# Attention: the first four turned tiles copied by ScalarE in two halves, each with its own signal

## The chip, the cores and the metric

The kernel runs on one core of a Trainium2 chip. The metric is the device time of one execution in microseconds, the median over runs. Before the change three runs gave 2184.6, 2189.52 and 2190.21 us, median 2189.52.

## What is computed

One encoder layer for two sequences of 272 and 1040 rows (16 meta rows are put ahead of 256 and of 1024), all in fp32. After a norm and a joint projection, one half of the width goes through a bidirectional RWKV-7 recurrence and the other through differential attention; both are projected, added, and followed by a gated feed-forward block. The part that matters here is the attention of 4 heads:

```python
s = jnp.einsum('bqhcd,bkhcd->bhcqk', qb, k)      # c = 0, 1: two score maps a head
pr = jax.nn.softmax(s, axis=-1)
amap = pr[:, :, 0] - lam * pr[:, :, 1]
return jnp.einsum('bhqk,bkhe->bqhe', amap, v)    # 128 columns of v
```

## The kernel before, in words

The stage is the function `attention`. A unit is 128 queries of one head. Each head has ten units: two of the short sequence (272 keys, "short units") and eight of the long one (1040 keys, "long units"), so there are 40 units, 8 short and 32 long, in the order short, short, long x8, four times over. Nothing reorders them: each engine runs a list of instructions written out by hand, and semaphores tie the lists together.

For unit k TensorE makes the two score maps (`score`, L1957) in two areas of PSUM, pS0 and pS1. VectorE takes the row maximum of each (`largest`, L2047), ScalarE the exponential with its row sum (`exp`, L2003: an ACTIVATE and a read of the accumulator), and VectorE the difference of the two maps (`difference`, L2054 to L2058), which gives the 128 x keys matrix in `pr`. For the product with v the keys must lie on the partitions, so TensorE turns the matrix in tiles of 128 x 128 (`turn`, L1970) into PSUM, from where the tiles are copied to `amT` in SBUF; then TensorE multiplies tile by tile with v and adds up in pO (`times_v`, L1980). Each fp32 matmul of `times_v` is recorded as two passes, each with a weight load.

A long unit has nine tiles in three batches, `tiles_of`: 0 to 3, 4 to 6, and 7 with 8 (tile 8 has 16 keys). Batch 0 is turned into the bank pT and copied by ScalarE (`turn_copy`, L1923 for full tiles, L1926 for the 16 keys of a short unit's last tile). Batches 2 and 1 are copied by VectorE (`tail`, the same lines): batch 2 from pT, batch 1 from the free end of pS0. A short unit has one batch of three tiles, copied by ScalarE with two instructions (two tiles, then 16 keys) and one signal behind the second.

TensorE's order in one turn of its loop is: scores of k (they need both exponentials of k - 1), batch 0 of k - 1 turned (needs the difference), product of batch 0 (needs ScalarE's copy and a free half of pO), batch 2 turned, batch 1 turned (needs the first exponential of k, since it writes into pS0), product of batch 2 (needs VectorE's copies), product of batch 1. ScalarE's order is: copy of batch 0 of k - 1, two exponentials of k, copy of the finished output of k - 1 (L2014). VectorE's order is: difference of k - 1, from unit 24 on one transpose of the solved inverse (L2068, L2070), two maxima of k, then the copies of batches 2 and 1 of k - 1.

Beside this, POOL works on the solve of the recurrence (`substitute`, L1032 to L1045) for the first part of the stage. The block of the next stage starts when all engines have left this one.

Of the kernel before, what the change touches and what calls it, by code (L numbers as in the profile page):

```python
# [26 lines left out]
P = 128  # L27
D = 1024
META = 16
LEN_A, LEN_B = META + 256, META + 1024  # L30
# [102 lines left out]
PRIMED = 2  # L133
# [1731 lines left out]
def attention(nc, g):  # L1865

    units = []
# [7 lines left out]
    units = [(h,) + u for h in range(HEADS) for u in units]  # L1875
    ALL = len(units)
    with Ctx(nc, "at") as c:
        ident = c.sb("ident", (P, P))
        pr = [[c.sb(f"pr{s}{x}", (P, LEN_B)) for x in range(2)] for s in range(2)]
        amT = [c.sb(f"amT{s}", (P, 9, P)) for s in range(2)]  # L1880
# [6 lines left out]
        pT, pO = c.ps("pT"), c.ps("pO")  # L1887
# [6 lines left out]
        turned, act_copied, tail_copied = c.sem("turned"), c.sem("act_copied"), c.sem("tail_copied")  # L1894
        tiles_of = [[range(0, 4), range(4, 7), range(7, 9)] if u[3] == LEN_B else [range(0, 3)] for u in units]
        batches = [len(x) for x in tiles_of]
        by_act = [min(n, 1) for n in batches]
        by_dve = [n - a for n, a in zip(batches, by_act)]
        bat0, act0, dve0 = ([sum(x[:k]) for k in range(ALL)] for x in (batches, by_act, by_dve))
        row_sum = lambda k, x: st[k % 2][:, 1, 1:2] if x else g.z0[:, units[k][0], k % NU:k % NU + 1]  # L1900
        out_cols = lambda k: slice(k % 2 * P, (k % 2 + 1) * P)

        AFTER = (0, 2, 1)

        def copied(eng, k, b):

            if b == 0:
                eng.wait_ge(act_copied, PRIMED + act0[k] + 1)
            else:
                eng.wait_ge(tail_copied, PRIMED + dve0[k] + AFTER[b])  # L1910

        def turned_tile(b, w):

            return pS[0][:, 2 * 512 + (w - 3) * P:2 * 512 + (w - 2) * P] if b == 1 else pT[:, w % 7 * P:(w % 7 + 1) * P]

        def copy_batch(copy, k, b):

            ln = units[k][3]
            tiles = tiles_of[k][b]
            full = min(tiles.stop, ln // P)  # L1920
            src = pS[0][:, 2 * 512 + P:3 * 512] if b == 1 else pT[:, :]
            n = full - tiles.start
            last = copy(amT[k % 2][:, tiles.start:full, :], src[:, 0:n * P].rearrange("p (w t) -> p w t", w=n))  # L1923
            if full < tiles.stop:
                kn = ln - full * P
                last = copy(amT[k % 2][0:kn, full, :], turned_tile(b, full)[0:kn, :])  # L1926
            return last

        with nc.Block() as block:
            @block.sync  # L1930
            def _(sp):
                c.prime(sp)
                sp.dma_start(ident[:, :], g.small_of("ident")).then_inc(ident_in, 16)
                sp.dma_start(lam[:, :], g.lambdas.partition_broadcast(P)).then_inc(lam_in, 16)
                for sem, n in g.solve_stored:
                    sp.wait_ge(sem, n)
                for q in (1, 3):
                    sp.dma_start(g.below_first[QUADS[q], :, :].rearrange("p u c -> p (u c)"), g.below[q // 2, :, 0]).then_inc(first_in, 16)
                sp.wait_ge(first_in, PRIMED + 32)
# [6 lines left out]
            @block.tensor  # L1946
            def _(pe):
                mm = nc.tensor.matmul

                def score(k):  # L1950
                    h, q0, a, ln, v0 = units[k]
                    for x in range(2):
                        pe.wait_ge(exped[x], PRIMED + k)
                    for lo in range(0, ln, 512):
                        hi = min(lo + 512, ln)
                        for x, rows in enumerate(HALVES):
                            last = mm(pS[x][:, lo:hi], g.qr[rows, h, q0:q0 + P], g.kr[rows, h, a + lo:a + hi],  # L1957
                                      start=True, stop=True)
                            if hi == ln:
                                last.then_inc(scores[x], 1)  # L1960

                def turn(k, b):
                    ln = units[k][3]
                    if b == 0:
                        pe.wait_ge(diffed, PRIMED + k + 1)
                    if b == 1 and k + 1 < ALL:
                        pe.wait_ge(exped[0], PRIMED + k + 2)
                    for w in tiles_of[k][b]:
                        kn = min(P, ln - w * P)
                        last = nc.tensor.transpose(turned_tile(b, w)[0:kn, :], pr[k % 2][0][:, w * P:w * P + kn], ident[:, :])  # L1970
                    last.then_inc(turned, 1)

                def times_v(k, b):
                    h, q0, a, ln, v0 = units[k]
                    if b == 0:
                        pe.wait_ge(ocopied, PRIMED + k - 1)
                    copied(pe, k, b)
                    for w in tiles_of[k][b]:
                        kn = min(P, ln - w * P)
                        last = mm(pO[:, out_cols(k)], amT[k % 2][0:kn, w, :], g.vt[0:kn, h, v0 + w, :],  # L1980
                                  start=(w == 0), stop=(w == tiles_of[k][min(1, batches[k] - 1)][-1]))
                    if b == min(1, batches[k] - 1):
                        last.then_inc(outs, 1)
                score(0)
                pe.wait_ge(ident_in, PRIMED + 16)
                for k in range(1, ALL + 1):
                    if k < ALL:
                        score(k)
                    if k:
                        turn(k - 1, 0)  # L1990
                        times_v(k - 1, 0)
                        if batches[k - 1] > 1:
                            turn(k - 1, 2)
                            turn(k - 1, 1)
                            times_v(k - 1, 2)
                            times_v(k - 1, 1)

            @block.scalar
            def _(act):
                def exp(k, x):  # L2000
                    ln = units[k][3]
                    act.wait_ge(maxed[x], PRIMED + k + 1)
                    nc.scalar.activation(pr[k % 2][x][:, 0:ln], pS[x][:, 0:ln], ACT.Exp,  # L2003
                                         bias=st[k % 2][:, x, 0:1], accum_out=row_sum(k, x)).then_inc(exped[x], 1)

                def turn_copy(k, b):
                    act.wait_ge(turned, PRIMED + bat0[k] + b + 1)
                    if b == 0:
                        act.wait_ge(outs, PRIMED + k - 1)
                    copy_batch(nc.scalar.copy, k, b).then_inc(act_copied, 1)  # L2010

                def out_of(k):
                    act.wait_ge(outs, PRIMED + k + 1)
                    nc.scalar.copy(g.o_rows[:, units[k][0], k % NU, :], pO[:, out_cols(k)]).then_inc(ocopied, 1)  # L2014
                for k in range(ALL + 1):
                    if k:
                        turn_copy(k - 1, 0)
                    if k < ALL:
                        exp(k, 0)
                        exp(k, 1)  # L2020
                    if k == 0:
                        act.wait_ge(lamb, PRIMED + 1)
                        nc.scalar.activation(lams[:, 0:2], lams[:, 0:2], ACT.Exp).then_inc(lamb, 1)
                    if k:
                        out_of(k - 1)
# [1230 lines left out]
```

## Time and profile before

| | |
|---|---|
| median of three runs | 2189.52 us |
| the profiled execution | 2189.49 us, span 2187.7 us |
| TensorE's mean granted clock | 0.952 |
| attention stage | from about 649 to 927 us of the span |
| TensorE, VectorE, ScalarE busy in 649 to 927 | 231.0, 201.9, 116.8 us of 278 |
| long unit that repeats | 7.08 us |
| ScalarE's copies of batch 0 | 40, of 372 to 586 ns |

The busy time is a mean over stages with different limits. Times in a timeline are from the span's start; an entry with "x8" merges eight instructions that follow each other in the same group, and its duration is the time they took together.

### The profile page before, as it was taken

What the parts mean: (1) busy time and instruction counts of PE and PEld (TensorE: products, weight loads), DVE (VectorE), ACT (ScalarE), POOL (GpSimd) and SP (SyncE); (2) the same over time, 40 slices, a digit from 0 to 9 for tenths busy, and PEclk for the clock granted to TensorE, in tenths of its full rate; (3) what the DMA queues carried; (4) which work ended last, traced back from release to release, by engine and by line L of the source; (5) the groups of instructions that cost most, each with busy time, mean ns of one, the idle gap of its engine ahead of it and who ended that gap; (6) DMA issues with size and microseconds to landing.
All of it is one profiled execution on the core that took longest, in us unless ns stands there. A gap on an engine that the chain in (4) does not pass through costs nothing. (4 is left out here: it accounts for less than half of the span.)

```text
span 2187.7 us, 40777 instructions
## 1 busy us (share of the span) xinstructions
PE 1998.1 (91%) x16199; PEld 1666.5 (76%) x16199; DVE 1426.5 (65%) x2329; ACT 959.5 (44%) x1790; POOL 348.1 (16%) x354
## 2 busy tenths in 40 slices
PE   5999999997768888878999698899999999999999
PEld 4666777776545555677887487899999999988887
DVE  5877667674866678766777646765555555557566
ACT  7454467773744444444444322422322333333433
POOL 0000000000019994074453200000000000000000
PEclk8999999998878999958999899899999999999999
DMA  4111157777940000029983543022222222295343
GB/s 180 66 45 49 62 205 260 255 264 273 291 145 1 1 1 1 7 87 187 198 179 93 184 133 135 29 105 88 105 81 87 89 93 81 90 352 168 100 147 109
DMA packets 152296, 274.88 MB, mean 126 GB/s; under 512 B 13264, under 2 KB 85840, under 8 KB 149936
## 3 DMA queue, kind: packets, MB, share of 16 engines
q1 hardware_dynamic: 152112, 272.34, 39.1%
q8 instruction: 127, 2.08, 0.4%
q14 instruction: 57, 0.47, 0.1%
HBM read 169.39 MB, written 99.93 MB: 123 GB/s over the span
## 5 line engine op out<-in xcount | busy, mean ns | idle before, releaser
L2964 DVE TENSOR_TENSOR ff_lefts<-normed_raw,ff_lefts 128x512 fp32r<-128x512 f32 x154 | 105.5, 686 | 98.3 <-ACT ff_lefts L2848 98.3
L224 PE MATMUL ff_acc<-right_t_low,ff_lefts 128*128 128x320 f32 x528 | 163.1, 309 | 0.0
L225 PE MATMUL ff_acc<-right_t_high,ff_lefts 128*128 128x320 f32 x528 | 163.1, 309 | 0.0
L223 PE MATMUL ff_acc<-right_t_high,ff_lefts 128*128 128x320 f32 x528 | 163.1, 309 | 0.0
L223 PE MATMUL ff_acc<-normed_nl 128*128 128x512 f32 x385 | 149.8, 389 | 0.0
L225 PE MATMUL ff_acc<-normed_nl,normed_nh 128*128 128x512 f32 x385 | 149.8, 389 | 0.0
L2848 ACT CAST ff_lefts<-normed_raw 128x512 fp32r<-128x512 f32 x154 | 93.5, 621 | 116.0 <-DMA normed_raw<-in_w_up 56.1
L1980 PE MATMUL at_pO<-heads_vt,at_amT 128*128 128x128 f32 (+1 forms) x624 | 104.5, 302 | 34.8 <-ACT at_amT L1923 24.5
L2874 ACT COPY normed_n<-ff_acc 128x640 f32<-128x640 f32 x66 | 45.8, 694 | 205.5 <-PE ff_acc L225 204.4
L1980 PEld LDWEIGHTS at_pO<-heads_vt,at_amT 128*128 128x128 f32 (+1 forms) x624 | 82.8, 195 | 60.9 <-issue 39.9
L3036 DVE TENSOR_TENSOR normed_nl<-normed_raw,normed_nh 128x640 fp32r<-128x640 f32 x77 | 63.4, 823 | 91.7 <-ACT normed_nh L2897 91.7
L2897 ACT CAST normed_nh<-normed_raw 128x640 fp32r<-128x640 f32 x77 | 56.2, 730 | 143.6 <-PE ff_acc L225 123.9
L223 PE MATMUL pj_acc<-parts_nh,pj_w0rest 128*128 128x512 f32 (+1 forms) x288 | 110.2, 383 | 7.1 <-DVE parts_nl L802 7.1
L223 PE MATMUL ff_acc<-normed_nh,ff_lefts 128*128 128x320 f32 x352 | 109.8, 312 | 7.5 <-DVE ff_lefts L2964 7.5
L224 PE MATMUL ff_acc<-normed_nl,ff_lefts 128*128 128x320 f32 x352 | 109.6, 311 | 0.0
L225 PE MATMUL ff_acc<-normed_nh,ff_lefts 128*128 128x320 f32 x352 | 109.6, 311 | 0.0
L223 PE MATMUL pj_acc<-parts_nh,pj_w1rest 128*128 128x512 f32 (+1 forms) x288 | 109.5, 380 | 0.0
L2047 DVE TENSOR_REDUCE at_st<-at_pS 128x1 f32<-128x1040 f32 (+1 forms) x80 | 82.6, 1074 | 37.7 <-PE at_pS L1957 37.6
L635 ACT COPY pj_raw<-pj_acc 128x512 f32<-128x512 f32 (+1 forms) x72 | 37.4, 522 | 156.9 <-PE pj_acc L225 155.5
L224 PE MATMUL pj_acc<-parts_nl,pj_w1high 128*128 128x512 f32 (+1 forms) x288 | 105.6, 367 | 0.0
L225 PE MATMUL pj_acc<-parts_nh,pj_w1high 128*128 128x512 f32 (+1 forms) x288 | 105.4, 366 | 0.0
L224 PE MATMUL pj_acc<-parts_nl,pj_w0high 128*128 128x512 f32 (+1 forms) x288 | 105.4, 366 | 0.0
(384 smaller groups left out, 5687.9 us busy)
## 6 DMA issues: line engine op xcount, KB each, us to landing
normed_raw<-dram_h SPq DMA_DIRECT2D x77, 320.0 KB, 3.0
ch_ops<-dram_sx SPq DMA_DIRECT2D x88, 256.0 KB, 5.1
dram_sx<-pr_sx SPq DMA_DIRECT2D x16, 1024.0 KB, 4.6
dram_h<-normed_spread_h SPq DMA_DIRECT2D x44, 320.0 KB, 2.3
pj_packed<-in_w_in SPq DMA_DIRECT2D x24, 512.0 KB, 4.9
heads_vt<-dram_ab SPq DMA_DIRECT2D x44, 256.0 KB, 5.4
normed_raw<-in_w_gate SPq DMA_DIRECT2D x22, 512.0 KB, 4.4
normed_raw<-in_w_up SPq DMA_DIRECT2D x22, 512.0 KB
```

The source lines that it names most:

```text
L223: nc.tensor.matmul(out, ll, rh, start=start, stop=False, skip_group_check=onto_kept)
L224: nc.tensor.matmul(out, lh, rl, start=False, stop=False, skip_group_check=onto_kept)
L225: return nc.tensor.matmul(out, lh, rh, start=False, stop=stop, skip_group_check=onto_kept)
L635: nc.scalar.copy(raw[p % 2][:, CUTS[n]:CUTS[n + 1]], acc[bank_of(i)][:, 0:widths[n]]).then_inc(copied, 1)
L1980: last = mm(pO[:, out_cols(k)], amT[k % 2][0:kn, w, :], g.vt[0:kn, h, v0 + w, :], start=(w == 0), stop=(w == tiles_of[k][min(1, batches[k] ...
L2047: nc.vector.reduce_max(st[k % 2][:, x, 0:1], pS[x][:, 0:ln], AX_X, negate=True).then_inc(maxed[x], 1)
L2848: nc.scalar.copy(lefts[:, q % LEFTS, 0, :], raw[:, y, QUARTER[p], :]).then_inc(high, 1)
L2874: nc.scalar.copy(in_two(to), got(y, p)).then_inc(kept, 1)
L2897: nc.scalar.copy(left_high[s], left_raw[s]).then_inc(left_cut, 1)
L2964: tt(lefts[:, q % LEFTS, 1, :], raw[:, y, QUARTER[p], :], lefts[:, q % LEFTS, 0, :].bitcast(F32), ALU.subtract).then_inc(low, 1)
L3036: tt(left_low[s], left_raw[s], left_high[s].bitcast(F32), ALU.subtract).then_inc(left_rest, 1)
```

## The change

ScalarE copies batch 0 in two instructions for long units also: tiles 0 and 1, then tiles 2 and 3, and signals after each. For short units the two instructions are those of before (tiles 0 and 1, then the 16 keys of tile 2), with a signal after each. TensorE waits for the first signal before tile 0 and for the second before tile 2. The counters follow; the helper `copied` is gone, its wait for the tail stands in `times_v`.

```diff
--- before.py
+++ after.py
@@ -1894,20 +1894,12 @@
         turned, act_copied, tail_copied = c.sem("turned"), c.sem("act_copied"), c.sem("tail_copied")
         tiles_of = [[range(0, 4), range(4, 7), range(7, 9)] if u[3] == LEN_B else [range(0, 3)] for u in units]
         batches = [len(x) for x in tiles_of]
-        by_act = [min(n, 1) for n in batches]
-        by_dve = [n - a for n, a in zip(batches, by_act)]
-        bat0, act0, dve0 = ([sum(x[:k]) for k in range(ALL)] for x in (batches, by_act, by_dve))
+        by_dve = [n - 1 for n in batches]
+        bat0, dve0 = ([sum(x[:k]) for k in range(ALL)] for x in (batches, by_dve))
         row_sum = lambda k, x: st[k % 2][:, 1, 1:2] if x else g.z0[:, units[k][0], k % NU:k % NU + 1]
         out_cols = lambda k: slice(k % 2 * P, (k % 2 + 1) * P)
 
         AFTER = (0, 2, 1)
-
-        def copied(eng, k, b):
-
-            if b == 0:
-                eng.wait_ge(act_copied, PRIMED + act0[k] + 1)
-            else:
-                eng.wait_ge(tail_copied, PRIMED + dve0[k] + AFTER[b])
 
         def turned_tile(b, w):
 
@@ -1974,8 +1966,11 @@
                     h, q0, a, ln, v0 = units[k]
                     if b == 0:
                         pe.wait_ge(ocopied, PRIMED + k - 1)
-                    copied(pe, k, b)
+                    if b:
+                        pe.wait_ge(tail_copied, PRIMED + dve0[k] + AFTER[b])
                     for w in tiles_of[k][b]:
+                        if w in (0, 2):
+                            pe.wait_ge(act_copied, PRIMED + 2 * k + w // 2 + 1)
                         kn = min(P, ln - w * P)
                         last = mm(pO[:, out_cols(k)], amT[k % 2][0:kn, w, :], g.vt[0:kn, h, v0 + w, :],
                                   start=(w == 0), stop=(w == tiles_of[k][min(1, batches[k] - 1)][-1]))
@@ -2007,7 +2002,14 @@
                     act.wait_ge(turned, PRIMED + bat0[k] + b + 1)
                     if b == 0:
                         act.wait_ge(outs, PRIMED + k - 1)
-                    copy_batch(nc.scalar.copy, k, b).then_inc(act_copied, 1)
+                    ln = units[k][3]
+                    nc.scalar.copy(amT[k % 2][:, 0:2, :], pT[:, 0:2 * P].rearrange("p (w t) -> p w t", w=2)).then_inc(act_copied, 1)
+                    if ln == LEN_B:
+                        last = nc.scalar.copy(amT[k % 2][:, 2:4, :], pT[:, 2 * P:4 * P].rearrange("p (w t) -> p w t", w=2))
+                    else:
+                        kn = ln - 2 * P
+                        last = nc.scalar.copy(amT[k % 2][0:kn, 2, :], pT[0:kn, 2 * P:3 * P])
+                    last.then_inc(act_copied, 1)
 
                 def out_of(k):
                     act.wait_ge(outs, PRIMED + k + 1)
```

## Rows read from the trace of the kernel before

**Rows 1.** The page: busy time by engine, and the chain that ended last, by line.
```profile
PE 1998.1 (91%) x16199; PEld 1666.5 (76%) x16199; DVE 1426.5 (65%) x2329; ACT 959.5 (44%) x1790; POOL 348.1 (16%) x354
...
PE ff_acc L223 12%; PE ff_acc L225 12%; PE ff_acc L224 12%; DVE ff_lefts L2964 0%; DVE normed_n L3062 0%; ACT ff_lefts L2848 0%
```

**Rows 2.** The waits, 649 to 927 us: engine and line, releaser, total us, times, longest.
```profile
PE at_pO L1980 <- ACT at_amT L1923: 24.5, 32, 0.8
...
PEld at_pO L1980 <- DVE at_amT L1926: 12.5, 32, 0.5
...
PE at_pO L1980 <- ACT at_amT L1926: 5.6, 8, 0.7
```

**Rows 3.** Windows of single units: us, busy by engine, PEclk, DMA share, GB/s.
```profile
708.07:715.15 7.08, 6.17 (x39) 4.22 (x39) 5.10 (x9) 3.21 (x6) 6.45 (x9) 1.00 0.00 0
...
730.87:739.27 8.40, 6.16 (x22) 3.52 (x22) 5.49 (x6) 3.03 (x7) 7.85 (x8) 0.64 0.00 0
739.27:747.65 8.38, 7.61 (x39) 5.66 (x39) 5.06 (x9) 3.08 (x7) 7.91 (x7) 0.75 0.01 2
...
866.82:874.33 7.51, 5.27 (x22) 3.06 (x22) 5.21 (x7) 3.04 (x7) 0.00 (x0) 0.77 0.00 0
```

**Rows 4.** The timeline of one long unit: start us, us, engine, line, idle before.
```profile
707.48 2.39 DVE L2047 TENSOR_REDUCE at_st<-at_pS 128x1 f32<-128x1040 f32 x2 [0.71 <-PE at_pS L1957]
...
708.07 0.58 ACT L1923 COPY at_amT<-at_pT 128x512 f32<-128x512 f32 x1 [2.37 <-PE at_pT L1970]
...
708.75 1.13 ACT L2003 ACTIVATE at_pr<-at_pS,at_st 128x1040 f32<-128x1040 f32 x1
708.77 0.97 PEld L1980 LDWEIGHTS at_pO<-heads_vt,at_amT 128*128 128x128 f32 x8 [0.98 <-issue]
708.80 1.13 PE L1980 MATMUL at_pO<-heads_vt,at_amT 128*128 128x128 f32 x8 [0.77 <-ACT at_amT L1923]
...
709.77 0.38 PE L1970 MATMUL at_pT<-at_ident,at_pr 128*128 128x128 f32 x2
709.78 0.19 ACT L2003 ACTIVATION_READ_ACCUMULATOR at_pr<-at_pS,at_st 128x1 f32 x1
...
710.02 0.55 PE L1970 MATMUL at_pS<-at_ident,at_pr 128*128 128x128 f32 x3
...
710.39 0.27 DVE L1926 COPY at_amT<-at_pT 16x128 f32<-16x128 f32 x1
...
710.61 0.56 DVE L1923 COPY at_amT<-at_pS 128x384 f32<-128x384 f32 x1
710.72 1.58 PEld L1980 LDWEIGHTS at_pO<-heads_vt,at_amT 128*128 128x128 f32 x10 [0.39 <-DVE at_amT L1926]
...
711.72 1.30 DVE L2058 SCALAR_TENSOR_TENSOR at_pr<-at_pr,at_st 128x1040 f32<-128x1040 f32 x1
```

**Rows 5.** The tile that the edit copies, whole trace: durations ns min/median/max, forms.
```profile
L1923 ACT COPY at_amT<-at_pT x40: 372/585/586, 657.9 to 922.5; 128x512 f32<-128x512 f32 x32, 128x256 f32<-128x256 f32 x8
```

**Rows 6.** The timeline of two short units after each other.
```profile
726.55 0.37 ACT L1923 COPY at_amT<-at_pT 128x256 f32<-128x256 f32 x1 [0.87 <-PE at_pT L1970]
726.82 0.25 ACT L1926 COPY at_amT<-at_pT 16x128 f32<-16x128 f32 x1
...
727.82 0.19 ACT L2003 ACTIVATION_READ_ACCUMULATOR at_pr<-at_pS,at_st 128x1 f32 x1
...
728.24 2.11 PE L1957 MATMUL at_pS<-heads_kr,heads_qr 64*128 64x512 f32 x12
...
734.17 4.02 PE L1957 MATMUL at_pS<-heads_kr,heads_qr 64*128 64x512 f32 x12 [1.54 <-ACT at_pr L2003]
```

**Rows 7.** The timeline at a transpose of the inverse, and the last work of POOL.
```profile
835.49 1.16 DVE L2070 STREAM_TRANSPOSE solved_by_row<-solved_inv 128x512 f32<-128x512 f32 x1
...
836.53 2.36 DVE L2047 TENSOR_REDUCE at_st<-at_pS 128x1 f32<-128x1040 f32 x2
...
845.16 0.31 POOL L1045 TENSOR_TENSOR solved_inv<-solved_inv,solved_solve_tmp 128x62 f32<-128x62 f32 x1
```

## Prediction

> **What bounds the kernel now.** The page first: TensorE is busy for 91% of the span and the chain that ended last runs on TensorE rows of the feed-forward stage [rows 1]. That chain says nothing of the attention stage, so I read this stage by itself: its waits, then the tile that the edit touches, then one long unit and the short units in order of time. In the stage (649 to 927 us) the waits show TensorE held before the product by ScalarE's copy, 24.5 us in 32 waits for the long units and 5.6 us in 8 for the short ones, and before the tail product by VectorE's small copy, 12.5 us in 32 [rows 2]. These are the waits of TensorE on another engine that come back in every unit with a size.
>
> The repeating long unit takes 7.08 us (708.07 to 715.15) [rows 3], and 22 or so of the 32 are like it. Let T = 708.07, the start of ScalarE's 128x512 copy. TensorE waits until T + 0.73 (matmul at 708.80), issues 8 passes, the two transposes of batch 2 at 709.77, waits for the first exponential (its accumulator read ends at 709.97) and turns batch 1 at 710.02, waits for VectorE's small copies (end 710.66), and issues the tail at 710.72 [rows 4]. The difference for the next turn is done at 711.72 + 1.30 = 713.02, more than a microsecond before the next turn [rows 4]. So one chain of TensorE's own work goes round the loop with gaps in it; a gap shortened ahead of the product counts if the two later gates let it through.
>
> **The change, part by part.**
> *The copy in halves.* A 128x512 copy takes 585 ns, a 128x256 one 372 ns, both on ScalarE from the same bank [rows 5]. The product now starts on the end of the first: 585 - 372 = 213 ns earlier in each of 32 long units, with the same two waits ahead of it. The extra instruction: a copy behind a 372 ns copy starts 0.27 us after it (726.55 to 726.82) [rows 6], so two halves end at T + 0.27 + 0.37 = T + 0.64 instead of T + 0.585.
>
> *What that does to the exponential behind it on ScalarE.* The first exponential starts at 708.75 = T + 0.68, just after VectorE's first maximum (half of the 2.39 us from 707.48, so about 708.68) [rows 4]. The second half leaves ScalarE at T + 0.64, and the next instruction may start some 0.10 before that (0.37 against a spacing of 0.27). The exponential stays where it is: 0. Bounds: -0 (no overlap at all: T + 0.27 becomes T + 0.37, exponential at about T + 0.78) to 0.10 us later.
>
> *The new wait at tile 2.* Queued behind it on TensorE is everything: the rest of the product, both turns, the tail. Loads in the product are spaced (0.97 - 0.19)/7 = 0.11 us [rows 4], so tile 2's first load, the third, would be due at T + 0.70 + 0.22 - 0.21 = T + 0.71. The signal: second half at T + 0.64, plus the 0.05 that lies between the accumulator read's end (709.97) and the transposes (710.02) [rows 4] = T + 0.69. Met, by 0.02 us. I take 0; the bound is the serial copy, end T + 0.74, release T + 0.80, a stall of 0.09, and a restart on top (below).
>
 What the rows show of a restart: eight loads span 0.97 us but eight matmuls 1.13, (1.13 - 0.28)/7 = 0.12 against 0.11, and the first matmul stands 0.03 behind its load, so about 0.1 us for a restart. If every tile 2 paid this, the sum below would be 32 x 0.1 = 3.2 us smaller; with the signal before the due load it is not.
>
> *The gates behind the product.* (1) Batch 2's transposes come 0.21 earlier, 709.56 to 709.94. (2) Batch 1's transposes wait for the first exponential, unchanged at 710.02; the gap before them grows by 0.21. (3) VectorE has finished its second maximum at 709.87 and so copies batch 2 at 709.98, not 710.19; it ends at 710.45, and the tail's first load may go at 710.51. TensorE's last of the three transposes starts at 710.02 + 0.55 - 0.27 = 710.30, its next slot is 710.41: the tail starts 0.21 earlier. (4) VectorE's 384-wide copy stays at 710.61 to 711.17, signal 711.22. The tail's loads take 1.58 us for ten [rows 4]; the seventh-last of them, six before the end, stood at 712.30 - 0.19 - 5 x 0.11 = 711.55 and is now due at 711.34. Met by 0.12. So what I feared, that turn 1 takes over, does not reach the tail: the tail was held by the small copies, and those move. Gain per long unit 0.213 us. 32 x 0.213 = 6.82.
>
> *Short units.* Their old signal came after the 16-row copy (starts 0.27, takes 0.25: T + 0.52); now after the first (T + 0.37), 0.15 less. Of eight, four are followed by another short one: there the next scores start at 728.24 and also need the second exponential, whose read ends at 728.01 [rows 6]; with the 0.14 that two waits cost (708.655 to 708.80) it is 728.15, so 0.09 each, 0.36 together. The other four are followed by a long unit; the scores after them wait 1.54 us for ScalarE [rows 6], which starts its exponentials by VectorE's maximum and not by the copy: 0.
>
> *Where cover is missing.* From unit 24 on VectorE transposes a part of the inverse between the difference and the maximum. At 835.49 it takes 1.16 and the maximum starts at 836.53 [rows 7], 0.52 before the copy at 837.05 where it is 0.60 in the plain unit; a start of TensorE 0.21 earlier finds it 0.29 late, and the batch-2 copy, behind both maxima, stays where it was. This happens when POOL's work stretches VectorE's difference, and POOL ends at 845.5 [rows 7]: about three units, -0.2 each = -0.6. In plain units the transposes have 0.3 us to spare even so. No wait of VectorE on POOL stands among the waits of the stage, and three to four microseconds at that point don't bring one: after 845.5 POOL's part is complete.
>
> Sum: 6.82 + 0.36 - 0.6 = 6.6 us off the stage. The next stages start behind it as before and move as a block. The profiled execution took 2189.49 us (span 2187.7 and 1.8 around it), the median of the three runs is 2189.52: the same. 2189.5 - 6.6 = **2182.9 us**, -0.30%.
>
> **The rivals.**
> *A. Tile 2 stalls.* The halves don't overlap, or the signal is later than 0.05: stall 0.09 and a restart of 0.1, so 0.02 left of 0.213 per long unit. 32 x 0.02 + 0.4 = 1 us: 2188.5; half of it, 2186. For: the margin is 0.02. Against: the 0.27 spacing was seen in every short unit.
> *B. The exponential takes the place.* If ScalarE's second half delays the first exponential by x, turn 1 and the tail's limit move by x; 0.10 is free. At x = 0.2 half the gain is gone: 3.3 us, 2186.2. For: turn 1 starts 0.05 after its read ends [rows 4], so it waits for it already. Against: the maximum, not the copy, starts it.
> *C. The clock gives more.* After each head's short units the granted clock falls to the lower level (1.2 of 2.4 GHz). In the second head the stretch from 730.87 (a short unit's product, a long one's scores) takes 8.40 us at 0.64, the long unit after it 8.38 at 0.75, so 6.0 + 4.2 = 10.2 us low; in the fourth head the same stretch, from 866.82, takes 7.51 at 0.77 (3.4 us low) and the next is plain [rows 3]. Two heads at the shorter spell would give 2 x (0.89 + 1.30) = 4.4 more: 2178.5. For: less idle TensorE in the unit that decides. Against: the gap of 1.54 us that precedes the fall stays. The runs before lie between 2184.6 and 2190.2. The skill's same page, "What's actually happening", says that where the transition falls depends on the phase of a count that runs by itself, so the same kernel varies.
> *D. The clock takes it, slower than before.* One mechanism: the gap before turn 1 grows by 0.21 and stands nearer to the others, and in the long units of a head the clock stays low. A long unit at the lower level costs up to 1.30 more (8.38 against 7.08, only part of it low) [rows 3]; from six such units on the gain is lost, two heads of eight make +20.8 - 6.6 = +14: 2204. Against: TensorE's busy share rises, 6.17 of 7.08 us [rows 3] to 6.17 of 6.87, and in no plain unit is the clock below 1.00.
>
> **How the numbers follow.** Forecast 0.64, A 0.11, B 0.08, C 0.12, D 0.05. A measurement of this kernel can tell about 0.3% (6.6 us) from no change, and the forecast lies on that bound: 0.37 faster, 0.27 same. With C faster, A and B same, D slower: faster 0.49, same 0.46, slower 0.05. The range from 2178.5 (C) to 2187.5 (most of A and B) leaves out D and the ends of A.
>
> **What would show it.** Right: the long unit's copy-to-copy distance is 6.87 instead of 7.08 us; 64 halves at 372 ns; the product 0.52 behind the first copy; TensorE's gap before turn 1 longer by 0.2 us; the exponential still 0.68 behind T; the stage some 6.6 us shorter, others unchanged. Wrong: a wait of TensorE on ScalarE's copy between tiles 1 and 2 (A), exponentials later than T + 0.78 (B), a unit distance still near 7.08, or a granted clock below 1.00 inside a head (D).

## The result and the profile after

In the first comparison seven runs of the changed kernel gave a median of 2173.82 us (2168.34 to 2180.26) against 2189.37 before (2184.6 to 2190.66, seven runs): 15.6 us less, ratio 0.9942, 95% interval 0.9924 to 0.996. The forecast was 2182.9 and a range down to 2178.5, so the time lies below the range. Four later sets of runs on other occasions gave 0.9965, 0.9951, 0.9957 and 0.9948. Over all runs the kernel before took 2185.5 us in the mean (141 executions) and the changed one 2176.0 (47): 9.5 us less, with a 95% interval of some 1.4 to either side; without the first comparison it is 9.1, give or take 1.5. So 6 of the first 15.6 us belong to the executions of that comparison. Some 4 of them lie in the kernel before, whose 2189.4 was high against its own mean, and 2 in the changed one. No later set repeated them, and what made them was not found. 9.5 us is what has to be explained.

The changed kernel's profiled execution took 2172.77 us, its span 2170.8. TensorE on the page, which answers to [rows 1]:

```profile
PE 1991.4 (92%) x16199; PEld 1659.2 (76%) x16199; DVE 1429.2 (66%) x2329; ACT 961.3 (44%) x1822; POOL 349.8 (16%) x354
```

The waits of the stage, as in [rows 2]. The wait before the product falls from 24.5 to 17.7 us in the same 32 waits, 0.213 each; the short units' wait falls from 5.6 to 4.4 in 8, 0.15 each. The wait before the tail product falls, and the one before turn 1 comes up:

```profile
PE at_pO L1975 <- ACT at_amT L2006: 17.7, 32, 0.6
...
PEld at_pS L1962 <- ACT at_pr L1998: 10.5, 28, 0.6
...
PEld at_pO L1975 <- DVE at_amT L1918: 6.9, 31, 0.5
...
PE at_pO L1975 <- ACT at_amT L2011: 4.4, 8, 0.6
```

One long unit, to be laid beside [rows 4]; T is now 710.59. The two halves start 0.26 apart and end at T + 0.37 and T + 0.64. The product starts at T + 0.51. The exponential stays at T + 0.68, turn 1 at T + 1.95. The tail goes at T + 2.43, where it was T + 2.65:

```profile
709.99 2.39 DVE L2049 TENSOR_REDUCE at_st<-at_pS 128x1 f32<-128x1040 f32 x2 [0.61 <-PE at_pS L1949]
710.59 0.37 ACT L2006 COPY at_amT<-at_pT 128x256 f32<-128x256 f32 x1 [2.37 <-PE at_pT L1962]
710.85 0.38 ACT L2008 COPY at_amT<-at_pT 128x256 f32<-128x256 f32 x1
711.07 0.97 PEld L1975 LDWEIGHTS at_pO<-heads_vt,at_amT 128*128 128x128 f32 x8 [0.76 <-issue]
711.10 1.13 PE L1975 MATMUL at_pO<-heads_vt,at_amT 128*128 128x128 f32 x8 [0.55 <-ACT at_amT L2006]
711.27 1.13 ACT L1998 ACTIVATE at_pr<-at_pS,at_st 128x1040 f32<-128x1040 f32 x1
...
712.07 0.38 PE L1962 MATMUL at_pT<-at_ident,at_pr 128*128 128x128 f32 x2
712.29 0.19 ACT L1998 ACTIVATION_READ_ACCUMULATOR at_pr<-at_pS,at_st 128x1 f32 x1
...
712.54 0.55 PE L1962 MATMUL at_pS<-at_ident,at_pr 128*128 128x128 f32 x3
...
712.70 0.27 DVE L1918 COPY at_amT<-at_pT 16x128 f32<-16x128 f32 x1
713.02 1.58 PEld L1975 LDWEIGHTS at_pO<-heads_vt,at_amT 128*128 128x128 f32 x10 [0.17 <-DVE at_amT L1918]
...
713.12 0.56 DVE L1915 COPY at_amT<-at_pS 128x384 f32<-128x384 f32 x1 [0.16 <-PE at_pS L1962]
...
714.24 1.48 DVE L2060 SCALAR_TENSOR_TENSOR at_pr<-at_pr,at_st 128x1040 f32<-128x1040 f32 x1
```

The same kernel in windows of units, as in [rows 3]. The plain unit takes 6.87 us. But the stretches behind the short units have changed too: in head 2 the one that took 8.40 us at a clock of 0.64 takes 7.53 at 0.78, and the long unit after it 6.87 at 1.00 instead of 8.38 at 0.75; in head 3 the stretch takes 6.35 us at 1.00:

```profile
710.59:717.46 6.87, 6.22 (x39) 4.23 (x39) 5.34 (x9) 3.28 (x8) 6.32 (x8) 1.00 0.00 0
...
732.77:740.30 7.53, 5.32 (x22) 3.30 (x22) 5.00 (x6) 3.04 (x7) 6.98 (x8) 0.78 0.00 0
740.30:747.17 6.87, 6.25 (x39) 4.23 (x39) 5.41 (x9) 3.14 (x7) 6.48 (x6) 1.00 0.01 2
796.82:803.17 6.35, 3.87 (x22) 2.45 (x22) 4.92 (x6) 3.04 (x8) 5.96 (x6) 1.00 0.01 1
860.01:867.67 7.66, 5.45 (x22) 3.08 (x22) 5.18 (x7) 3.04 (x7) 0.00 (x0) 0.78 0.01 2
```

The whole attention stage, from the first score to the last product, in windows; before, then after. 277.3 us at a clock of 0.92 against 265.4 at 0.95, 11.9 less. The busy time of TensorE falls by 4.2 us with the same 1352 matmuls recorded: that is clock, not work.

```profile
649.62:926.94 277.32, 231.03 (x1352) 155.56 (x1352) 201.91 (x320) 116.16 (x249) 181.21 (x188) 0.92 0.01 3
```

```profile
653.40:918.79 265.39, 226.83 (x1352) 151.77 (x1352) 203.56 (x320) 118.05 (x281) 183.13 (x188) 0.95 0.01 3
```

The rest of the 16.9 us between the two spans lies behind the stage (stage of the solve's end 3.7, chunks 5.7, less the 3.8 by which its attention stage starts later). The later profiles do not repeat the 5.7: the chunks' stage takes 233.8, 232.1, 232.9 and 228.2 us in four profiles of the kernel before, 228.1, 231.8, 231.0, 229.1 and 231.6 in five of the changed one.

### The profile page after: what moved, and what is told of

The parts are those of the page before. It is cut to its first block and busy times, and to the rows that moved or that the text cites. A ratio compares the mean times of both kernels' runs of the same rounds, so it can differ in the third digit from the quotient of the medians.

```text
span 2170.8 us, 40809 instructions
## 1 busy us (share of the span) xinstructions
PE 1991.4 (92%) x16199; PEld 1659.2 (76%) x16199; DVE 1429.2 (66%) x2329; ACT 961.3 (44%) x1822; POOL 349.8 (16%) x354
## 5 line engine op out<-in xcount | busy, mean ns | idle before, releaser
L1975 PE MATMUL at_pO<-heads_vt,at_amT 128*128 128x128 f32 (+1 forms) x624 | 102.2, 297 | 23.2 <-ACT at_amT L2006 17.7
L225 PE MATMUL pj_acc<-parts_nh,pj_w0high 128*128 128x512 f32 (+1 forms) x288 | 105.3, 366 | 0.0
```

The source lines that it names most:

```text
L225: return nc.tensor.matmul(out, lh, rh, start=False, stop=stop, skip_group_check=onto_kept)
```

## The experiments

**Is it the kernel or the execution?** Both kernels were run and profiled again without an edit, the old one three times and the new one four times.

> The kernel before, unchanged, for a second profile. Theory M+S (the shorter copy wait gives 7.1 us, and the stretches at the lower clock that follow each head's short units get shorter because of it): second and third head again hold a spell of about 10 us each, attention stage (first scores to last product) 276 to 278 us. Theory M+P (7.1 us from the wait, the rest is where the clock's changes happen to fall in one execution): spells at the head starts differ from the first profile, each 3 to 10 us in any head, stage anywhere between 271 and 278 us. Both: long unit 7.08 us, total near 2189.

> The changed kernel again. M+S: spells of at most 3.4 us at the head starts, as in its first profile (2 spells in heads 2 to 4), stage 265 to 266 us. M+P: longer spells appear too, stage anywhere between 264 and 270 us. Both: long unit 6.87 us, total 2168 to 2180, with the granted clock and the time moving against each other from run to run.

> The kernel before, third profile. The two before it had stretches of 10.2, 10.2 and 3.4 us below 1.00 at heads 2, 3 and 4 and a stage of 277.3 us. If these lengths belong to the kernel's own spacing of work, the same again within 2 us. If the phase is free, heads with 0 to 7 us appear and the stage ranges from 271 to 280.

> The changed kernel, third profile. The two so far: 3.4, 0, 3.4 (stage 265.4) and 6.9, 3.4, 6.9 with one more at the end (270.1). Theory S: always shorter in total than the 24 us of before, stage 265 to 270. Theory P: also a profile with 20 us or more, stage 272.

> The kernel before, fourth profile: as for the third. Together with the third it gives the mean of the granted clock and of the time over some 50 executions against which the changed kernel is set.

> The changed kernel, fourth profile. Over all executions, theory M alone (the waits' 7.1 us) makes the mean 7 us lower than before at an equal mean clock; theory M+S makes it 9 to 10 us lower, with the mean granted clock up by 0.001 to 0.002; the first comparison's 15.6 would have to come back if the change did more than both say.

> The changed kernel on the same chip: stage 265 to 270 us, 9 us below before (2176). This is the yardstick for the version with three pieces.

What each profile shows, from its clock record and its units (us of the stretches below 1.00 at heads 2, 3, 4; all time below 1.00 in the stage; stage from first score to last product):

```
kernel    profile   at heads 2, 3, 4    low in all   stage us   run set's ratio to before
before    first     10.2  10.2  3.4     42.6         277.3      -
before    e1        10.2  10.2  3.4     42.5         277.3      0.9997 (0.9983 to 1.0011)
before    e9        10.2  10.2  3.4     42.7         277.4      0.9999 (0.998 to 1.0018)
before    e11       10.2  10.2  3.4     42.8         277.5      0.9998 (0.9984 to 1.0012)
changed   first      3.4   0    3.4     25.5         265.4      0.9942 (0.9924 to 0.996)
changed   e2         6.8   3.4  6.8     43.2         270.1      0.9965 (0.9948 to 0.9981)
changed   e10        6.8   3.4  0       29.1         266.2      0.9951 (0.993 to 0.9973)
changed   e12        6.8   3.4  0       40.7         269.4      0.9957 (0.9938 to 0.9976)
changed   e15        3.4   0    3.4     30.5         267.2      0.9948 (0.993 to 0.9966)
```

The kernel before does the same each time: its stretches begin 83.5 to 83.8 us after the stage's first score and are equally long in all four. The changed kernel's, added up, are shorter in all five, with more scatter. Its e2, e12 and e15 hold other low time at the stage's start or end, so that over the whole stage e2 is low for as long as the kernel before. The mean stage is 277.4 before and 267.7 after, 9.7 us less, which agrees with the 9.5 of the times. Its time below 1.00 falls from 42.6 to 33.8 us in the mean. So the shorter stretches at the heads are the kernel's own and not the luck of one execution; only the excess of the first set was. Of the two theories in the expectations, M+P fails on the kernel before, whose pattern is fixed. M+S fails in its size on the changed one: e2 has stretches of 6.8 us and a stage of 270.1, where M+S allowed 3.4 and 266.

**Is it the early start or the split?** Both halves are copied, but the product waits for the second.

```diff
-                        if w in (0, 2):
-                            pe.wait_ge(act_copied, PRIMED + 2 * k + w // 2 + 1)
+                        if w == 0:
+                            pe.wait_ge(act_copied, PRIMED + 2 * k + 2)
```

> Two halves as in the changed kernel, but the product waits for the second before tile 0. Theory 1 (the early start alone brings the gain): the product starts 0.06 to 0.07 us later than before the change (second half ends at T + 0.65 instead of 0.585), long unit 7.15 us, time 2 us above before, 2191. Theory 2 (the split itself frees something, a shorter ScalarE instruction for example): long unit below 7.08, time below before.

Its timeline: the product starts at T + 0.79, and the unit takes 7.14 us, as theory 1 has it.

```profile
681.60 0.37 ACT L2006 COPY at_amT<-at_pT 128x256 f32<-128x256 f32 x1 [2.37 <-PE at_pT L1962]
681.87 0.38 ACT L2008 COPY at_amT<-at_pT 128x256 f32<-128x256 f32 x1
...
682.39 1.13 PE L1975 MATMUL at_pO<-heads_vt,at_amT 128*128 128x128 f32 x8 [0.83 <-ACT at_amT L2008]
```

The time was 2184.74 us, ratio 0.999 (0.9972 to 1.0008), so the 2 us could not be seen as a loss. The reason is in its windows: at head 2 it has no stretch at the lower clock at all, at heads 3 and 4 the full 10.2. The stretch after the short units at 1.00, and the same at 0.64:

```profile
733.08:739.12 6.04, 3.80 (x22) 2.46 (x22) 4.47 (x6) 3.03 (x8) 5.73 (x5) 1.00 0.00 0
797.71:806.12 8.41, 6.16 (x22) 3.52 (x22) 4.88 (x6) 3.04 (x8) 7.94 (x7) 0.64 0.00 1
```

This is the price of a stretch without any guess: 6.04 against 8.41, and for the long unit behind it 7.08 against 8.38. A 10.2 us stretch costs 3.7 us. And a kernel whose units are slower, not busier, lost one: where a head's start comes to lie in time matters. This speaks for the shift of the changed kernel's heads (1.9, 5.9 and 10.6 us earlier behind the first score at heads 2, 3 and 4) as the cause of its shorter stretches, and not for TensorE's higher share.

The clock records of the twelve profiles without a filler say more. Measured from the moment when TensorE goes idle in the gap ahead of the first long scores of a head, the fall of the clock comes

```
0.5 to 1.0 us later    14 stretches, all of 10.2 us (8 of the kernel before, e3's 2, e4's 3, and e15's first head)
1.1 to 2.6 us later    21 stretches, all of 3.4 us
2.8 to 3.0 us later     5 stretches, all of 6.8 us
```

In the changed kernel the falls at heads 2 to 4 come 1.2 to 3.0 us behind the start of the gap. At head 2 of the first pair the fall stands where it stood (83.6 and 83.5 us after the first score), but the gap starts at 81.0 instead of 83.0. The gap itself did not get shorter, it grew by 0.12:

```profile
736.04 3.18 PE L1949 MATMUL at_pS<-heads_kr,heads_qr 64*128 64x512 f32 x12 [1.66 <-ACT at_pr L1998]
```

So the length of a stretch goes with the place of the fall against the gap, in all the kernels alike. No run moved the heads and changed nothing else, so that the shift is the cause stays an inference from this regularity and from e3.

**The short units alone.**

```diff
+                    if ln == LEN_B:
+                        nc.scalar.copy(amT[k % 2][:, 0:4, :], pT[:, :]...).then_inc(act_copied, 2)
+                    else:
                         nc.scalar.copy(amT[k % 2][:, 0:2, :], ...).then_inc(act_copied, 1)
                         nc.scalar.copy(amT[k % 2][0:kn, 2, :], ...).then_inc(act_copied, 1)
...
+                        if w == 0:
+                            pe.wait_ge(act_copied, PRIMED + 2 * k + (2 if ln == LEN_B else 1))
+                        if w == 2 and ln != LEN_B:
+                            pe.wait_ge(act_copied, PRIMED + 2 * k + 2)
```

> Only the short units' first signal is early; the long units copy 512 columns in one instruction as before. Theory 1: 4 x 0.09 = 0.4 us from the waits, total 2189. If the short units' earlier start were what shortens the slow-clock spells at the head starts (M+S through the short units): one or two of the 10 us spells become 3.4 us and the stage is 2 to 4.5 us shorter. If it is the long units' start: spells as before, stage 277.

The short unit's gain is as forecast: the next scores come 1.08 us after the product's start at 728.54 and 1.60 after the copy, where it was 1.69 [rows 6].

```profile
728.54 1.10 PE L1977 MATMUL at_pO<-heads_vt,at_amT 128*128 128x128 f32 x6 [0.55 <-ACT at_amT L2013]
...
729.62 0.70 PE L1949 MATMUL at_pS<-heads_kr,heads_qr 64*128 64x512 f32 x2
```

But the kernel was slower than before, by 0.2%: 2190.1 us, ratio 1.0018 (1.0002 to 1.0034), stage 280.3. Two causes stand in its profile. Head 4 has a 10.2 us stretch too now (10.2, 10.2, 10.2), though the copy of its second short unit begins only 0.4 us later behind the first score than before (217.6 against 217.2 us). The fall there comes 1.0 us behind the start of the gap, where it comes 1.1 to 1.25 in the four profiles of the kernel before. And the long unit takes 7.12 us: its copy starts 0.74 us after the four transposes begin, where the kernel before needs 0.69 (707.38 to 708.07 there):

```profile
687.40 0.66 PE L1962 MATMUL at_pT<-at_ident,at_pr 128*128 128x128 f32 x4
...
688.14 0.59 ACT L2009 COPY at_amT<-at_pT 128x512 f32<-128x512 f32 x1 [2.41 <-PE at_pT L1962]
```

The only differences there are the increment of two at once and the way the source is written; which of them costs the 0.045 us was not tried. So this run is not a clean half of the change, and for the short units it says only the 0.09.

**The clock out of the way.** TensorE is given work in the gap that precedes the falls.

```diff
                 for k in range(1, ALL + 1):
+                    if 2 < k < ALL and k % NU == 3:
+                        for _ in range(6):
+                            mm(pT[:, 0:P], ident[:, :], ident[:, :], start=True, stop=True)
                     if k < ALL:
                         score(k)
```

> The kernel before, with six matmuls of the identity by itself (12 passes, about 1.3 us at the full clock, written where nobody reads) put into TensorE's gap of 1.54 us after the second short unit of each head, ahead of the long scores that wait for ScalarE. It tests whether that gap makes the clock fall. If it does: no stretch below 1.00 starts at heads 2 to 4, each 10.2 us stretch gives back about 3.6 us (8.40 + 8.38 against 6.04 + 7.08) and the 3.4 us one 1.5, stage 277.3 - 8.8 = 268.5, time about 8 us below before. If it does not: stretches as before, stage 277 to 280.

> The changed kernel with the same filler. With the clock at 1.00 at heads 2 to 4 in both, the stage is to be shorter than in the kernel before with the filler by the wait's share alone. Theory M (7.1 us: 32 x 0.213 + 4 x 0.09, less 0.1): stage 261.4, and the time 7 us below that of the kernel before with the filler. Theory S (the change itself makes the clock's stretches shorter, worth 4 us or more): with the filler that part is gone, so the difference of the two filled kernels is clearly smaller than that of the two plain ones.

> The kernel before with the filler again. Stage 266.8 as in its first profile, no stretch below 1.00 at heads 2 to 4, time 9 us below before.

> The changed kernel with the filler again. If the clock's share is what the change brings beside the waits: stage 260 to 261 and a time 6 to 7 us below the kernel before with the filler. If the filled pair again differs by only 2 us in time while the stages differ by 6, something behind the stage gives part of it back (the stage with the chunks took 236 us there against 231).

The kernel before with the filler, head 2: twelve passes end just before the scores, which start 3.31 us after the copy as they did (3.30), so the filler costs nothing:

```profile
726.05 1.10 PE L1980 MATMUL at_pO<-heads_vt,at_amT 128*128 128x128 f32 x6 [0.70 <-ACT at_amT L1926]
...
727.07 1.60 PE L1989 MATMUL at_pT<-at_ident 128*128 128x128 f32 x12
...
728.69 2.12 PE L1957 MATMUL at_pS<-heads_kr,heads_qr 64*128 64x512 f32 x12
```

And its windows: the stage, the stretch, the long unit behind it. No clock below 1.00 at any head but the first, the stage takes 266.8 us instead of 277.3, the stretch 6.04, the unit 7.08:

```profile
645.74:912.52 266.78, 226.16 (x1400) 154.63 (x1400) 203.14 (x320) 116.51 (x249) 182.94 (x188) 0.97 0.01 3
725.38:731.42 6.04, 5.33 (x34) 3.87 (x34) 4.26 (x6) 3.04 (x7) 5.68 (x5) 1.00 0.00 0
731.42:738.50 7.08, 6.14 (x39) 4.22 (x39) 5.78 (x9) 3.22 (x6) 6.66 (x6) 1.00 0.01 2
```

Without the gap of 1.54 us after the short units the clock does not fall at heads 2 to 4. The gap alone does not decide it: unfilled, the clock fell behind it in 12 places of 12 in the kernel before, but in 11 of 15 in the changed one. Filled, the stage gives back 10.5 us, where 8.8 was expected: the filler stands in the first head too, and the stretch of 3.4 us there (from 18.7 us after the first score) is gone as well. The changed kernel with the filler:

```profile
651.17:912.03 260.86, 227.83 (x1400) 155.10 (x1400) 203.91 (x320) 118.20 (x281) 183.51 (x188) 0.97 0.01 3
```

The stages of the filled pair differ by 5.9 us (266.8 and 260.9), in the second pair by 4.4 (266.4 and 262.0). The times: 2176.87 and 2173.46, then 2182.11 and 2173.33; in the mean over both sets 2179.2 (20 executions) and 2173.9 (12), 5.3 us apart, give or take 2.6. (The single sets give 2.4, give or take 3.5, and 7.1, give or take 3.1.) So with the clock equal the change is worth 4 to 6 us, and the other 4 to 5 of its 9.7 are the clock's: plain, the stage before pays 277.4 - 266.6 = 10.8 us for the clock, the changed one 267.7 - 261.4 = 6.3. Expected were 7.1 for the waits; that they bring less is explained below. Less of the filler's gain reaches the end of the kernel. The kernel before got 0.9964 (0.9945 to 0.9983) in the first set and 0.9988 (0.9972 to 1.0004) in the second, 5.3 us in the mean (give or take 2.5) of its 10.8, where 8 and 9 were expected; the changed kernel some 2 of its 6.3. The chunks' stage took 230.9 and 235.3 us in the one, 236.2 and 234.0 in the other, against a mean of 231.8 and 230.3 without the filler. Why it grows behind a filled attention stage was not tried and stays open.

**Smaller first pieces.** Tile 0, tile 1, then tiles 2 and 3.

```diff
-                    nc.scalar.copy(amT[k % 2][:, 0:2, :], pT[:, 0:2 * P]...).then_inc(act_copied, 1)
+                    for w in range(2):
+                        nc.scalar.copy(amT[k % 2][:, w, :], pT[:, w * P:(w + 1) * P]).then_inc(act_copied, 1)
...
-                        if w in (0, 2):
-                            pe.wait_ge(act_copied, PRIMED + 2 * k + w // 2 + 1)
+                        if w < 3:
+                            pe.wait_ge(act_copied, PRIMED + 3 * k + w + 1)
```

> The changed kernel with the copy in three pieces: tile 0, tile 1, tiles 2 and 3 (short units: tile 0, tile 1, the 16 keys), a signal after each. A 128-wide copy takes 0.27 us against 0.37, so the product starts 0.10 earlier still, at T + 0.41. If nothing else holds: 6.77 us a long unit. But VectorE ends its second maximum at T + 1.80, so the batch 2 copy starts at T + 1.83 at best against 1.90 now: 6.80 us, 2 us off the changed kernel. Rival: the third piece comes at T + 0.70 and the wait at tile 2 or the later exponential (due at T + 0.68) takes it back: 6.87 or more.

> Three pieces and the filler together. If both work: stage 261.4 - 2.2 = 259.2 us, time about 2 us below the changed kernel with the filler and 17 below the kernel before.

> Three pieces and the filler again: stage 259.5 us as in its first profile (unit 6.76), so 8 us under the changed kernel's mean stage of 267.8; time 2170 or somewhat less if all of it reaches the end, 2172 as in its first six executions if the later stages keep some.

The unit takes 6.76 us, 0.11 less than with halves. The product starts at T + 0.41 (689.47). Turn 1 stays at T + 1.96 and now holds TensorE (0.20 <- the exponentials' read), and the tail follows it directly at T + 2.35: here the exponential has taken the place. VectorE's copy of batch 2 too now starts as its second maximum ends (688.47 + 2.39 = 690.86). By this timeline a still earlier product would bring nothing; it was not tried.

```profile
688.47 2.39 DVE L2050 TENSOR_REDUCE at_st<-at_pS 128x1 f32<-128x1040 f32 x2 [1.21 <-PE at_pS L1949]
...
689.06 0.43 ACT L2007 COPY at_amT<-at_pT 128x128 f32<-128x128 f32 x2 [2.36 <-PE at_pT L1962]
689.38 0.39 ACT L2009 COPY at_amT<-at_pT 128x256 f32<-128x256 f32 x1
...
689.47 1.13 PE L1975 MATMUL at_pO<-heads_vt,at_amT 128*128 128x128 f32 x8 [0.45 <-ACT at_amT L2007]
...
690.86 0.29 DVE L1915 COPY at_amT<-at_pT 128x128 f32<-128x128 f32 x1
...
691.02 0.55 PE L1962 MATMUL at_pS<-at_ident,at_pr 128*128 128x128 f32 x3 [0.20 <-ACT at_pr L1998]
...
691.41 1.30 PE L1975 MATMUL at_pO<-heads_vt,at_amT 128*128 128x128 f32 x6
```

Three pieces alone gave 2173.2 us (ratio 0.9941, 0.9922 to 0.9959). With the filler the stage takes 259.5 and 259.6 us in the two profiles,

```profile
652.74:912.23 259.49, 224.50 (x1400) 154.69 (x1400) 204.42 (x320) 119.92 (x321) 183.44 (x188) 0.97 0.01 3
```

and the times were 2171.98 and 2171.34, ratios 0.9934 (0.9915 to 0.9954) and 0.9939 (0.9917 to 0.9961). In the same set as the second the changed kernel had 2175.27, too near to tell apart by those runs alone; over all executions the version with three pieces and the filler is 4.3 us below the changed kernel, give or take 2.4. It is the fastest version measured, but from three pieces without the filler it can't be told apart (1.0 us, give or take 3). Of the 8 us that its stage is shorter, the chunks' stage took some back (235.3 and 238.5 us); 17 us below the kernel before were expected, and it was 12.

## Why the prediction was wrong

**Right: the mechanism of the plain unit, to the hundredth.** 0.213 us from the shorter first copy, second half at T + 0.64, exponential unmoved, tile 2 not stalled, turn 1 unmoved but not deciding, the tail held by VectorE's small copies and released 0.21 earlier, 6.87 us. Rivals A and B did not happen. The feared restart of 0.1 us at tile 2, 3.2 us in all, did not come: the eight loads still take 0.97 us and the eight matmuls 1.13, as in [rows 4]. So a wait that is met in time costs nothing here. The Trainium skill, "TensorE: Matmul & The Clock Gate", Step-by-step, says that weight loads are pulled ahead of matmuls in flight; that a wait would cost something by this was my own inference, and no run here has a wait inside a run of loads that is not met in time.

**Right for a wrong reason: the margin at tile 2.** The prediction took tile 2's first load for the third and found it due at T + 0.71, 0.02 us behind the signal. But every tile has two passes, each with a load, so tile 2's first load is the fifth: it was due at T + 0.70 + 4 x 0.11 - 0.21 = T + 0.93, and came at T + 0.92 (711.07 + 4 x 0.11 = 711.51). The margin was 0.23 us. Rival A would not have come even without any overlap of the halves (signal at T + 0.80); its chance of 0.11 rested on this misreading. With three pieces the fifth load came at T + 0.82 and the signal some 0.06 before it, again without a stall.

**Right: the short units.** From copy to copy 4.32 us became 4.23 in heads 2 to 4, the forecast 0.09; in the first head, where the clock is low, it can't be read. Ahead of a long unit it was 0.03 (6.04 against 6.01 in the filled kernels, forecast 0).

**Wrong: "32 x 0.213".** Four long units are followed by a short one, whose scores are brief. There the next turn comes soon and waits for VectorE's difference. The kernel before, at the end of head 1: the difference ends at 718.81 + 1.41 = 720.22 and the transposes start at 720.27.

```profile
718.81 1.41 DVE L2058 SCALAR_TENSOR_TENSOR at_pr<-at_pr,at_st 128x1040 f32<-128x1040 f32 x1
...
720.27 0.42 PEld L1970 LDWEIGHTS at_pT<-at_ident,at_pr 128*128 128x128 f32 x4 [0.47 <-DVE at_pr L2058]
```

The changed kernel at the same place: the difference ends at 722.41, the transposes start at 722.47. The wait of their weight loads has grown from 0.47 to 0.58 us, and so takes back half of what was gained.

```profile
721.11 1.30 DVE L2060 SCALAR_TENSOR_TENSOR at_pr<-at_pr,at_st 128x1040 f32<-128x1040 f32 x1
...
722.47 0.42 PEld L1962 LDWEIGHTS at_pT<-at_ident,at_pr 128*128 128x128 f32 x4 [0.58 <-DVE at_pr L2060]
722.47 0.66 PE L1962 MATMUL at_pT<-at_ident,at_pr 128*128 128x128 f32 x4 [0.15 <-DVE at_pr L2060]
```

These units gained 0.10, 0.23, less than nothing and nothing in the first pair, 5.71 us being the floor in both kernels. That is 0.5 to 0.9 us too much in the sum; I had read the timeline of a unit in mid-head and multiplied it. The "-0.6" for the units where POOL stretches the difference was 0.1 in the profile after (one unit of 6.98 instead of 6.87) and 0.7 in e15 (7.20, 7.05 and 7.09). With 28 x 0.213 = 6.0, 0.3 and 0.1 from the short ones, and POOL's share off, 6 us are left, and the filled pairs measured 5.9 and 4.4. The second pair differs from the first at the stage's start: up to the copy of the first long unit the changed kernel gained 0.2 us in the first pair and lost 1.1 in the second. Behind that copy they gained 5.7 and 5.4.

**Wrong: the clock as a chance of 0.12 instead of a term.** This is the step that failed. The sum holds nothing for the clock, for the reason given against Rival C: "the gap of 1.54 us that precedes the fall stays". It stayed, at 1.66 us, and the fall mostly stayed too, but how long the clock stays down goes with where the fall comes against the gap, and the earlier start moved that. The runs show 4 to 5 us in its place: the stages differ by 9.7 us as they are and by 5.9 and 4.4 with the gap filled. Rival C named the mechanism and a size (4.4 more, 2178.5). At heads 2 to 4 it happened in all five profiles, 6.8 to 17.0 us low instead of 23.8; over the whole stage its worth varies, since e2 has as much low time as the kernel before. Which way a shift goes can't be told from the profile of before alone: the kernel with the short units alone, shifted by 0.4 us, came out with a third long stretch. The price of Rival C was right for what it prices, a stretch of 10.2 us that becomes one of 3.4 (3.7 less 1.5 is 2.2 us); it left out that a stretch can be gone altogether, as in four of the changed kernel's fifteen places. The Trainium skill's sentence that the place of the transition depends on a window that runs by itself (same page, "What's actually happening"), which I used to call the stretches variable, does not fit the kernel before: four profiles, one pattern. The changed kernel does vary, with three patterns in five profiles. The measurement decides.

**Not a step of the mechanism:** the last 6 us of the first comparison. The forecast was counted down from 2189.5, the median of three runs, and the kernel's mean over 141 executions is 2185.5. Counted from the same 2189.5, a gain of 9.5 us gives 2180.0, inside the range; what put the first time below it is this scatter. The range of 9 us was drawn for the mechanism and left little for runs of this kernel, which spread over 20 us (2173 to 2194 for the kernel before over all sets).

## What to carry to other kernels

When a wait is shortened in a loop, follow the unit through every gate, but do it once for each kind of neighbour: the units at a seam have other gates than those in the middle. Where the profile shows stretches at the lower clock that return at the same place, look for the gap that precedes them and price it against the same unit at full clock: filling it with idle matmuls takes three lines and gave the stage here as much as the change did (10.8 us against 9.7), though only about 5 of it reached the end. Where a matmul is recorded in two passes, count the loads by tile before you place a wait between them. And compare whole times of a kernel with such stretches over tens of executions, or compare the stage in the profiles.

## What was not expected of the hardware

The low stretches of one kernel were the same, in place and length, in four executions out of four (83.5 to 83.8 us behind the first score, 10.2 us). Over twelve profiles of five kernels the length of a stretch went with the place of its fall: 10.2 us where the fall came 0.5 to 1.0 us after TensorE went idle, 3.4 where it came 1.1 to 2.6 us after, 6.8 where it came 2.8 to 3.0 after. A twelve-pass filler (1.60 us in its row) between a product and the scores behind it kept the granted clock at 1.00 through heads 2 to 4 in all six profiles that had it. And a 512-wide copy on ScalarE that counts its semaphore up by two began 0.045 us later than the one that counts by one; whether the count is the cause stays open.
